# A widened 256-byte tile, one modulation vector moved to the tensor engine, and a gate unit moved into attention

## The chip, the cores and the metric

The kernel runs on one core of a Trainium2 chip. The metric is device microseconds of one execution, the median over the runs of a kernel. All arithmetic is in fp32, and the large matmuls use the fp32r form (one pass over split operands, see below).

## The reference

Two layers (DEPTH = 2) over 256 latent tokens x and 256 context tokens ctx, D_MODEL = 1024. Both streams pass layer 0; in layer 1 the context only gives keys and values. Cut to what matters here:

```
sh1, sc1, g1, sh2, sc2, g2 = split(silu(c) @ w_mod[l] + b_mod[l], 6)     # the same for c_ctx
xn   = rmsnorm(h, norm1_g[l]) * (1 + sc1) + sh1
proj = xn @ w_in[l]                  # pool | hyena | q | kv | gates ga, gb, gc (3 x 1024)
a    = pool_mixer(proj) @ pool_out
b    = hyena_mixer(proj) @ hy_out
cm   = attention(8 heads; latents read ctx and latent keys) @ w_o
h    = h + g1 * ((sigmoid(ga) * a + sigmoid(gb) * b + sigmoid(gc) * cm) @ w_out)
h    = h + g2 * (square(relu((rmsnorm(h, norm2_g[l]) * (1 + sc2) + sh2) @ w_ff1)) @ w_ff2)
```

So each layer needs six modulation vectors of 1024 numbers, each a product of a 1 x 1024 vector (per stream) with a 1024 x 1024 block of w_mod. The kernel numbers them 0 to 11 over both layers.

## The kernel before, in words

**Units.** Every large weight is cut into units of 128 x 1024 numbers (512 KB); there are 272, `PHASES` gives each phase its first unit `g0` and its count `mains`. SP loads a unit into one of four slots of `raw`; ScalarE copies it rounded into `wh` (line 750), VectorE writes the remainder `raw - wh` into `wl` (line 1078). That pair is called the split of the unit, done `AHEAD = 3` units before the unit is multiplied. TensorE multiplies a unit as 24 matmuls: for each of 8 blocks of 128 rows, high weight by high activation, high by low, low by high (`three`, lines 1629 to 1631). The activations are kept as such pairs too: `xh`/`xl` (the normed input), `hid_h`/`hid_l` (hidden layer of the MLP), `fh`/`fl` (attention output, pooled and hyena mix), `cqh`/`cql`, `ckh`/`ckl` (latents), `uh`/`ul`. A matmul has 512 columns in layer 0 (both streams) and 256 in layer 1.

**Tiles.** Tiles are placed one behind the other in the order of their `alloc` lines; the first starts at byte 8320 of a partition and each start is rounded up to 32 bytes. `h`, `xh`, `xl`, `raw`, `wh`, `wl` come first and start at multiples of 64 bytes. Then comes `picks`, `(36,)` floats (144 bytes), and behind it all other tiles; they start 32 bytes past a multiple of 64. In layer 1, `xh`, `xl`, `fh`, `fl`, `hid_h` and `hid_l` are read 192 bytes (3 x 64) further on (`by_layer`).

**Modulation vectors.** Vectors 0 and 1 are made at the start, the other ten in 80 units of w_mod (8 a vector), woven into the phases by the pattern strings in `_phases`: M is a main unit, m a modulation unit behind it, t one in the tail of the phase, s the sum of a weighed vector. A modulation unit on TensorE (`mod_unit`, line 1658) is four concurrent matmuls of 32 stationary columns. The vectors named in `SUMMED = (7, 8, 9)` are instead weighed on VectorE (`weigh`, lines 1099 and 1102: weight times the number of the partition, added into an accumulator in `gained` or `final`), and TensorE only sums the accumulator over the partitions with `picks` (`mod_sum`, line 1670). After either, ScalarE copies the rows ("copy", `copy_mod`), TensorE turns them ("turn", `turn_mod`, line 1677) and VectorE adds the bias (`add_mod`, line 1107). The tail units of `w_out` and of layer 0's `ff2b` run while the norm that follows is computed: TensorE does the squares' sum (`rms`), then the tail; meanwhile ScalarE takes the root, VectorE the reciprocal (line 1134), the products (line 1156) and the remainders `xl` (line 1163), and TensorE then starts the next phase with two units interleaved block by block (`wave`). Layer 0's `ff2b` has 8 tail units, all of them (`GAP_SLOTS`) loaded beforehand into free tiles, four of them into the room of `xl`, so that the first product of the norm waits for those four (`GAP_XL_LAST`).

**Attention.** The third gate has 8 units; `gate_c0` (4) stands before the projections uq and ukv, `gate_c1` (4) right before attention. ScalarE drains each gate unit by a sigmoid into `sig`, from PSUM banks 0 and 1. Attention has 16 jobs in layer 0 (8 heads x 2 streams; the context's see 256 keys) and 8 in layer 1. A job is: scores (line 1976), maxima on VectorE (1380), exponentials on ScalarE (960), division on VectorE (1387, 1390), transposes on TensorE (1987), copies on ScalarE (971); every two jobs one product with the values (`weighted_values`, 2002) into bank `pair % 2`, which VectorE drains to `fh`/`fl` (1401, 1402). In the last two jobs no scores are left to put between. Then comes `wo` (4 units in two halves of 12 matmuls each; VectorE drains by line 1427), then `pool`.

Of the kernel before, what the change touches and what calls it, by code (L numbers as in the profile page):

```python
# [7 lines left out]
KB = D // 128  # L8
# [49 lines left out]
def _phases():  # L58


    out = []
    for layer in range(DEPTH):
        first = layer == 0

        def with_mods(pattern):
            return pattern if first else pattern.replace("m", "").replace("t", "").replace("s", "")
        out += [(layer, *p) for p in [
            ("q", "MMM"), ("kv", "MM"), ("kpe", "M"),
            ("gate_c0", "MMMM"),
            ("uq", "MMM"), ("ukv", "MM"), ("gate_c1", "MMMM"),  # L70
            ("wo", with_mods("MMmmMMmm")),
            ("pool", with_mods("MMmmMMmm")),
            ("gate_a0", with_mods("MMmm")), ("gate_a1", with_mods("MMmmM")), ("pool_w", "M"),
            ("gate_a2", with_mods("MMmmMmm")), ("pool_out", "MMMM"),
            ("hy", with_mods("MMmmMMmmMMmmMMmmMMMM")), ("gate_b0", "MMM"), ("gate_b1", "MMM"), ("gate_b2", "MM"),
            ("hy_out", "MMMM"),
            ("w_out", "MMMMMMMM" + (16 if first else 8) * "t"),
            ("ff1a", with_mods("MMMMMMMMMMMMMMMM")), ("ff2a", with_mods("MmMmMmMmMmMmMmMmMmMmMmMmsMmMmMmMm")),
            ("ff1b", 16 * "M"), ("ff2b", with_mods("MmMmMmMmsMmMmMmMmMMMMsMMMM" + 8 * "t")),
        ]]  # L80
    return out
# [22 lines left out]

SUMMED = (7, 8, 9)

# [55 lines left out]
def load_order(order):  # L162
# [3 lines left out]
    for kind, i in order:  # L166
# [5 lines left out]
        else:  # L172
# [4 lines left out]
            else:  # L177
# [10 lines left out]
GAP_FREE = {"w_out": "hy_out", "ff2b": "ff2b"}  # L188
GAP_SLOTS = {i: (layer, name, slot) for layer, name, count in ((0, "w_out", 14), (0, "ff2b", 8), (1, "w_out", 6))
             for slot, i in enumerate(gap_units(layer, name, count))}  # L190
GAP_COUNTS = {(0, "w_out"): 14, (0, "ff2b"): 22, (1, "w_out"): 28}
GAP_XL_LAST = max(i for i, (_, name, slot) in GAP_SLOTS.items() if name == "ff2b" and slot < 4)
# [42 lines left out]
def backbone(nc, x_in, units_in, pairs_in, mod_units_in, params_in, consts_in, fwd_in, inv_in, counts_in, emb_in, f_w12_in,  # L235
# [5 lines left out]
    with ctx:  # L241
# [23 lines left out]
        wl = alloc(ctx, "wl", (SLOTS, 1024), R)  # L265
        picks = alloc(ctx, "picks", (36,))
        sq_sum = alloc(ctx, "sq_sum", (T,))
# [138 lines left out]
        with ExitStack() as s:  # L406
# [5 lines left out]
        weighted_of = {7: gained[:, :, :].rearrange("p a b -> p (a b)").rearrange("p (s c) -> p s c", c=D),  # L412
                       8: final[:, 0:1, :], 9: final[:, 1:2, :]}

# [6 lines left out]
        def latent_bank(i):  # L421

            p = PHASES[1, "q"]
            return (2 + p.dve0 % 2, 2 + (p.dve0 + 1) % 2, 6, 0, 1)[i]

        def pooled_bank(p, g):
# [306 lines left out]
        def _(act):  # L733
# [87 lines left out]
            def gates(layer, b, rest=None):  # L821
                p = PHASES[layer, "gate_" + b]
                n = width(layer)
                m0 = GATE_PARTS[b]
                for j in range(p.mains):
                    split(p.g0 + j + AHEAD)
                    act.wait_ge(unit_done, p.g0 + j + 1)
                    act.activation(sig[:, m0 + j, 0:n], ps[:, (p.act0 + j) % 2, 0:n], ACT.Sigmoid).then_inc(act_bank_free, 1)  # L828
                    if rest is not None:
                        rest(p, j)  # L830
                    mod_events(p, j)
# [92 lines left out]
            for layer in range(DEPTH):  # L924
# [39 lines left out]
                for jb, (hd, s) in enumerate(jobs):  # L964
                    if jb + 1 < len(jobs):
                        exponentials(jb + 1)
                    act.wait_ge(transposed[layer], jb + 1)
                    if jb >= 3:
                        act.wait_ge(pv_done[layer], (jb - 1) // 2)
                    for half in range(2 if jobs[jb][1] == 0 else 1):  # L970
                        act.activation(probs_t[jb % 3][:, 2 * half:2 * half + 2, :],
                                       ps[:, 6 + half, :].rearrange("p (k q) -> p k q", q=SEQ), ACT.Copy).then_inc(pt_act[layer], 1)
                for _ in straight(layer, "wo"):
                    pass
# [89 lines left out]
        def _(dve):  # L1064
# [44 lines left out]

            def loop(layer, name, drain=None):  # L1110
                p = PHASES[layer, name]
                for j in range(p.mains):
                    split(p.g0 + j + AHEAD)
                    if drain is not None:
                        drain(p, j)
                    mod_events(p, j)
# [158 lines left out]
            for layer in range(DEPTH):  # L1275
# [83 lines left out]
                for b in range(2):  # L1359
                    dve.tensor_tensor(roped[:, 0, b, :], q_pe[:, b, 0:SEQ], cos[:, :], ALU.mult)  # L1360
                    chained(dve.tensor_tensor(roped[:, 1, b, :], ps[:, 6, b * SEQ:(b + 1) * SEQ], sin[:, :], ALU.mult))
                    for i in range(4):
# [5 lines left out]
                        else:  # L1368
                            chained(done)
                loop(layer, "gate_c1")  # L1370

# [21 lines left out]
                def outputs(jb):  # L1393

                    hd, s = jobs[jb]
                    if hd % 2:
                        pair = jb // 2
                        dve.wait_ge(pv_done[layer], pair + 1)
                        src = ps[:, pair % 2, 0:SEQ]
                        t = slice(s * SEQ, (s + 1) * SEQ)  # L1400
                        chained(dve.tensor_copy(fh_of[layer][:, hd // 2, t], src))
                        dve.tensor_tensor(fl_of[layer][:, hd // 2, t], src, fh_of[layer][:, hd // 2, t].bitcast(F), ALU.subtract)\
                           .then_inc(o_ready[layer], 1)
# [11 lines left out]
                for jb in range(len(jobs) - 2, len(jobs)):  # L1415
                    outputs(jb)

                def branch_out(name, b):
# [207 lines left out]
        def _(pe):  # L1626
# [94 lines left out]

            def loop(layer, name, main, j0=0):
                p = PHASES[layer, name]
                for j in range(j0, p.mains):
                    pe.wait_ge(lo_ready, p.g0 + j + 1)
# [52 lines left out]
            def gates(layer, b, rest=None):  # L1778
                n = width(layer)

                def main(p, j):
                    bank = act_bank(p, j)
                    blocks(ps[:, bank, 0:n], (p.g0 + j) % SLOTS, xh_of[layer], xl_of[layer], n).then_inc(unit_done, 1)
                    if rest is not None:
                        rest(j)
                loop(layer, "gate_" + b, main)

# [98 lines left out]
            for layer in range(DEPTH):  # L1886
# [103 lines left out]
                def weighted_values(pair):  # L1990
# [4 lines left out]
                    if pair == 0:  # L1995
                        pe.wait_ge(act_bank_free, drained(layer, "gate_c1"))
                    elif pair >= 2:
                        pe.wait_ge(o_ready[layer], pair - 1)
                    pe.wait_ge(pt_act[layer], copies(jb + 1))
                    for kb in range(nb):  # L2000
                        for half in range(2):
                            mm = pe.matmul(ps[64 * half:64 * half + 64, pair % 2, 0:SEQ],  # L2002
                                           v_t[:, tb0 + kb, (hd - 1 + half) * VH:(hd + half) * VH],
# [3 lines left out]
                def copies(jb):  # L2007

                    return 2 * min(jb, HEADS) + max(jb - HEADS, 0)

                pe.wait_ge(q_ready, layer + 1)
# [8 lines left out]
                for jb in range(len(jobs)):  # L2020
                    if jb + 2 < len(jobs):
                        scores(jb + 2)
                    transposes(jb)
                    if jb >= 2 and jb % 2 == 0:
                        weighted_values(jb // 2 - 1)
                weighted_values(len(jobs) // 2 - 1)

# [7 lines left out]

                branch_out("wo", o_ready[layer], HEADS // 2 * (ns - 1))
                for j, p, slot in straight(layer, "pool"):
                    bank = act_bank(p, j)
# [276 lines left out]
```

## Time and profile before

| | us |
|---|---|
| median of 3 runs | 1378.83 (1377.84 to 1378.91) |
| profiled execution | 1376.82 |
| its span, first to last instruction | 1375.0 |
| TensorE busy | 1344.5 (98%) |
| VectorE busy | 818.0 (59%) |
| ScalarE busy | 550.3 (40%) |
| GpSimd busy | 198.3 (14%) |
| mean DMA rate | 149 GB/s |

The granted clock of TensorE is 0.998 of full speed over the span. A row of a timeline gives the start in us from the span's start, the duration, the engine, the line, the operation, the tiles it writes and reads, and, in brackets, idle time before it and what ended it. Matmuls overlap, so what a matmul costs the stream is the distance from its start to the start of the next, not its duration.

### The profile page before, as it was taken

To read this page: it belongs to the slowest core of one execution; us is meant where nothing else is said; L and a number is where in the kernel's file an instruction comes from. 1 tells how busy PE (TensorE), PEld (TensorE's weight loads), DVE (VectorE), ACT (ScalarE), POOL (GpSimd) and SP (SyncE) were. 2 spreads that over 40 slices of the span, in tenths; PEclk is the share of its full clock that TensorE was granted. 3 is DMA by queue.
4 is the path that set the end of the run, shared out by engine and by line. 5 is a ranking of instruction groups with operands and counts; after the bars stand their busy time and mean duration, and the time that the engine had idled before them with its cause. 6 is when DMAs were issued, how large, how long until landed. Compare 5 with 4: busy or idle time off the path is not lost.

```text
span 1375.0 us, 19372 instructions
## 1 busy us (share of the span) xinstructions
PE 1344.5 (98%) x7918; PEld 1104.8 (80%) x7918; DVE 818.0 (59%) x1163; ACT 550.3 (40%) x852; POOL 198.3 (14%) x177
## 2 busy tenths in 40 slices
PE   8999999999999999999999999999999999999998
PEld 3567766777777886888878887788779999899998
DVE  5576574234448666545644445378865788765663
ACT  6652462332233323443113331144555445553553
POOL 1261000703100142000000002300004404100012
PEclk9999999999999999999999999999999999999999
DMA  9342204444531363223553337314225647455552
GB/s 373 135 144 92 107 1 148 155 173 149 209 110 57 127 245 123 99 101 125 192 185 111 105 140 269 114 51 156 94 92 179 228 137 281 148 186 186 185 185 77
DMA packets 55433, 205.27 MB, mean 149 GB/s; under 512 B 6277, under 2 KB 6661, under 8 KB 53808
## 3 DMA queue, kind: packets, MB, share of 16 engines
q1 hardware_dynamic: 52848, 193.70, 40.5%
q0 software_dynamic: 2208, 9.81, 1.9%
q8 instruction: 63, 1.03, 0.3%
q10 hardware_dynamic: 288, 0.52, 0.1%
q14 instruction: 26, 0.21, 0.1%
HBM read 200.86 MB, written 3.15 MB: 148 GB/s over the span
## 4 chain that ended last, share of the span: by engine, by line
PE 89%; DVE 5%; ACT 2%; DMA 1%; issue 1%; SPq 0%; POOL 0%; DVEq 0%; ACTq 0%
PE ps L1629 27%; PE ps L1630 26%; PE ps L1631 26%; PE ps L1976 2%; DVE wl L1078 2%; PE ps L1987 1%; PE ps L2002 1%; DMA pairs<-in_pairs 1%; PE ps L1658 1%; PE ps L2074 1%; PE ps L2086 1%; PE ps L1818 1%; PE ps L1697 1%; DVE rstd L1134 1%; DVE k_t L1352 0%
## 5 line engine op out<-in xcount | busy, mean ns | idle before, releaser
L1629 PE MATMUL ps<-xh,wh 128*128 128x512 f32 (+2 forms) x1392 | 473.0, 340 | 2.9 <-DVE xl L1163 2.0
L1630 PE MATMUL ps<-xl,wh 128*128 128x512 f32 (+2 forms) x1392 | 465.4, 334 | 0.0
L1631 PE MATMUL ps<-xh,wl 128*128 128x512 f32 (+2 forms) x1392 | 465.4, 334 | 0.0
L1078 DVE TENSOR_TENSOR wl<-raw,wh 128x1024 fp32r<-128x1024 f32 (+2 forms) x272 | 353.4, 1302 | 175.2 <-ACT wh L750 172.2
L750 ACT ACTIVATE wh<-raw 128x1024 fp32r<-128x1024 f32 (+2 forms) x272 | 283.8, 1044 | 313.2 <-PE ps L1631 312.8
L1629 PEld LDWEIGHTS ps<-xh,wh 128*128 128x128 f32 (+1 forms) x1392 | 261.1, 188 | 43.9 <-issue 14.0
L1631 PEld LDWEIGHTS ps<-xh,wl 128*128 128x128 f32 (+1 forms) x1392 | 260.5, 187 | 29.2
L1630 PEld LDWEIGHTS ps<-xl,wh 128*128 128x128 f32 (+1 forms) x1392 | 260.2, 187 | 28.3 <-issue 1.2
L1629 PE MATMUL ps<-hid_h,wh 128*128 128x512 f32 (+1 forms) x512 | 174.5, 341 | 0.0
L1630 PE MATMUL ps<-hid_l,wh 128*128 128x512 f32 (+1 forms) x512 | 173.8, 339 | 0.0
L1631 PE MATMUL ps<-hid_h,wl 128*128 128x512 f32 (+1 forms) x512 | 173.3, 338 | 0.0
L1631 PEld LDWEIGHTS ps<-hid_h,wl 128*128 128x128 f32 x512 | 96.9, 189 | 11.7
L1629 PEld LDWEIGHTS ps<-hid_h,wh 128*128 128x128 f32 x512 | 96.1, 188 | 12.7 <-issue 1.2
L1630 PEld LDWEIGHTS ps<-hid_l,wh 128*128 128x128 f32 x512 | 96.3, 188 | 11.5
L1600 DVE TENSOR_TENSOR relu<-relu 128x512 f32<-128x512 f32 (+1 forms) x64 | 35.7, 559 | 98.9 <-ACT relu L1045 98.9
L1045 ACT ACTIVATE relu<-ps 128x512 f32<-128x512 f32 (+1 forms) x64 | 31.4, 491 | 140.7 <-PE ps L1631 140.7
L1577 DVE SCALAR_TENSOR_TENSOR h<-ps,mods,h 128x256 f32<-128x256 f32 x72 | 32.6, 481 | 88.9 <-PE ps L1631 88.8
L651 POOL TENSOR_TENSOR y<-y,gated 128x512 f32<-128x512 f32 (+1 forms) x32 | 36.3, 1142 | 257.7 <-DVE gated L1427 257.5
L828 ACT ACTIVATE sig<-ps 128x512 f32<-128x512 f32 (+1 forms) x48 | 23.5, 491 | 122.2 <-PE ps L1631 122.2
L637 POOL TENSOR_TENSOR sq_sum<-h 128x512 f32<-128x512 f32 (+1 forms) x4 | 5.2, 1298 | 453.7 <-DVE h L1577 453.7
L1629 PE MATMUL ps<-fh,wh 128*128 128x512 f32 (+1 forms) x192 | 66.0, 344 | 1.0 <-DVE gated L1427 0.9
L1631 PE MATMUL ps<-fh,wl 128*128 128x512 f32 (+1 forms) x192 | 65.1, 339 | 0.0
(273 smaller groups left out, 1467.2 us busy)
## 6 DMA issues: line engine op xcount, KB each, us to landing
raw<-in_units SPq DMA_DIRECT2D x262, 512.0 KB, 3.3
mod_ring<-in_mod_units SPq DMA_DIRECT2D x52, 512.0 KB, 4.1
gap_hy<-in_mod_units SPq DMA_DIRECT2D x15, 512.0 KB, 4.8
pairs<-in_pairs SPq DMA_DIRECT2D x6, 1024.0 KB, 14.2
raw<-in_units SPq DMA_DIRECT2D x6, 384.0 KB, 3.1
h<-in_x SPq DMA_DIRECT2D x4, 512.0 KB, 7.8
mod_ring<-in_pairs SPq DMA_DIRECT2D x2, 1024.0 KB, 15.8
counts<-in_counts POOLq DMA_DIRECT2D x2, 1024.0 KB, 5.1
```

Source lines behind the costliest of these rows:

```text
L651: pool.tensor_tensor(y[:, m, 0:n], y[:, m, 0:n], gated[:, m % 2, 0:n], ALU.add).then_inc(y_added[layer], 1)
L750: act.activation(wh[:, g % SLOTS, 0:n], raw[:, g % SLOTS, 0:n], ACT.Copy).then_inc(hi_ready, 1)
L828: act.activation(sig[:, m0 + j, 0:n], ps[:, (p.act0 + j) % 2, 0:n], ACT.Sigmoid).then_inc(act_bank_free, 1)
L1045: act.activation(relu[:, j % 2, 0:n], ps[:, (p.act0 + j) % 2, 0:n], ACT.Relu).then_inc(act_bank_free, 1)
L1078: dve.tensor_tensor(wl[:, g % SLOTS, 0:n], raw[:, g % SLOTS, 0:n], wh[:, g % SLOTS, 0:n].bitcast(F), ALU.subtract)\
L1134: dve.reciprocal(rstd[:, t], rstd[:, t]).then_inc(rstd_ready, 1)
L1577: last = dve.scalar_tensor_tensor(h[:, m, t], ps[:, bank, t], mods[:, gate, m, s:s + 1], h[:, m, t], ALU.mult, ALU.add)
L1600: dve.tensor_tensor(relu2[:, j % 2, 0:n], relu[:, j % 2, 0:n], relu[:, j % 2, 0:n], ALU.mult)\
L1629: pe.matmul(dst, w_h, m_h, start=first, stop=False)
L1630: pe.matmul(dst, w_h, m_l, start=False, stop=False)
L1631: return pe.matmul(dst, w_l, m_h, start=False, stop=last)
L1976: pe.matmul(ps[:, S_BANKS[2 * (jb % 2) + qb], 0:keys], q_t[0:QK, hd, q0:q0 + 128], k_t[0:QK, hd, k0:k0 + keys], start=True, stop=True).the ...
```

## The change

Three things:

1. `picks` is 64 floats (256 bytes) instead of 36, so every tile behind it starts 96 bytes later, at a multiple of 64.
2. `SUMMED` is (7, 8). Vector 9 goes through TensorE as 8 modulation units, three of them inside layer 0's `ff2b` and five in its tail, which has 13 units (11 of them in prepared room, the first of which for `xl`'s room is the tail's third). The copies and turns of vectors 9 and 10 fall into layer 1's first phases.
3. The fourth unit of `gate_c1` leaves its place before attention. It is multiplied in pieces into bank 0: four blocks (12 matmuls) before the transposes of the last job but one, then in layer 0 two blocks before the last job's transposes and two behind them, in layer 1 four behind them. The product of the last pair but one goes to bank 4. ScalarE takes its sigmoid behind the attention's copies, and the split of unit `g0 + 6` (the third of `wo`) comes on ScalarE and on VectorE behind attention.

```diff
-            ("ff1b", 16 * "M"), ("ff2b", with_mods("MmMmMmMmsMmMmMmMmMMMMsMMMM" + 8 * "t")),
+            ("ff1b", 16 * "M"), ("ff2b", with_mods("MMMsMmmMMMmMMMMMMMMM" + 13 * "t")),
-SUMMED = (7, 8, 9)
+SUMMED = (7, 8)
-GAP_SLOTS = {i: (layer, name, slot) for layer, name, count in ((0, "w_out", 14), (0, "ff2b", 8), (1, "w_out", 6))
+GAP_SLOTS = {i: (layer, name, slot) for layer, name, count in ((0, "w_out", 14), (0, "ff2b", 11), (1, "w_out", 6))
...
-        picks = alloc(ctx, "picks", (36,))
+        picks = alloc(ctx, "picks", (64,))
...
+        def output_bank(layer, pair):
+
+            return 4 if pair == HEADS // 2 * (width(layer) // SEQ) - 2 else pair % 2
...
                 for j in range(p.mains):
+                    if b == "c1" and j == p.mains - 1:
+                        return
                     split(p.g0 + j + AHEAD)
...
+                act.wait_ge(unit_done, PHASES[layer, "gate_c1"].g0 + 4)
+                act.activation(sig[:, KB - 1, 0:n], ps[:, 0, 0:n], ACT.Sigmoid).then_inc(act_bank_free, 1)
+                split(PHASES[layer, "gate_c1"].g0 + 3 + AHEAD)
                 for _ in straight(layer, "wo"):
...
-                loop(layer, "gate_c1")
+                loop(layer, "gate_c1", count=3)
...
                 for jb in range(len(jobs) - 2, len(jobs)):
                     outputs(jb)
+                split(PHASES[layer, "gate_c1"].g0 + 3 + AHEAD)
...
                     if pair == 0:
-                        pe.wait_ge(act_bank_free, drained(layer, "gate_c1"))
+                        pe.wait_ge(act_bank_free, drained(layer, "gate_c1", 3))
+                    elif pair == len(jobs) // 2 - 2:
+                        pe.wait_ge(exp_done[layer], 2 * (len(jobs) - 1))
...
+                def last_gate(at, count):
+
+                    p = PHASES[layer, "gate_c1"]
+                    if at == 0:
+                        pe.wait_ge(lo_ready, p.g0 + 4)
+                        pe.wait_ge(o_ready[layer], len(jobs) // 2 - 3)
+                    mm = blocks(ps[:, 0, 0:n], (p.g0 + 3) % SLOTS, xh_of[layer], xl_of[layer], n, k0=at, count=count,
+                                first=at == 0, last=at + count == KB, at=128 * at)
+                    if at + count == KB:
+                        mm.then_inc(unit_done, 1)
...
                     if jb + 2 < len(jobs):
                         scores(jb + 2)
+                    if jb == len(jobs) - 2:
+                        last_gate(0, 4)
+                    elif jb == len(jobs) - 1 and layer == 0:
+                        last_gate(4, 2)
                     transposes(jb)
                     if jb >= 2 and jb % 2 == 0:
                         weighted_values(jb // 2 - 1)
+                if layer == 0:
+                    last_gate(6, 2)
+                else:
+                    last_gate(4, 4)
                 weighted_values(len(jobs) // 2 - 1)
...
                 branch_out("wo", o_ready[layer], HEADS // 2 * (ns - 1))
+                pe.wait_ge(act_bank_free, drained(layer, "gate_c1"))
```

## Rows read from the trace of the kernel before

**Rows 1.** The page: busy time by engine; the chain that ended last.
```profile
PE 1344.5 (98%) x7918; PEld 1104.8 (80%) x7918; DVE 818.0 (59%) x1163; ACT 550.3 (40%) x852; POOL 198.3 (14%) x177
...
PE 89%; DVE 5%; ACT 2%; DMA 1%; issue 1%; SPq 0%; POOL 0%; DVEq 0%; ACTq 0%
```

**Rows 2.** Timeline of TensorE, layer 0, ff1b into ff2b (start, duration, operation).
```profile
801.23 0.39 PE L1629 MATMUL ps<-xh,wh 128*128 128x512 f32 x1
...
812.11 0.40 PE L1629 MATMUL ps<-hid_h,wh 128*128 128x512 f32 x1
...
817.73 0.39 PE L1629 MATMUL ps<-hid_h,wh 128*128 128x512 f32 x1
```

**Rows 3.** Timeline of TensorE, layer 0, values of ukv (weights as moving tile).
```profile
134.93 0.40 PE L1630 MATMUL ps<-wl,ckh 128*128 128x512 f32 x1
...
137.27 0.40 PE L1631 MATMUL ps<-wh,ckl 128*128 128x512 f32 x1
```

**Rows 4.** Timeline of TensorE, layer 1, first matmuls of units: gate_c1; ff2a, ff1b.
```profile
973.96 0.28 PE L1629 MATMUL ps<-xh,wh 128*128 128x256 f32 x1
...
976.68 0.28 PE L1629 MATMUL ps<-xh,wh 128*128 128x256 f32 x1
...
1271.98 0.28 PE L1629 MATMUL ps<-hid_h,wh 128*128 128x256 f32 x1
...
1274.86 0.28 PE L1629 MATMUL ps<-xh,wh 128*128 128x256 f32 x1
...
1277.68 0.28 PE L1629 MATMUL ps<-xh,wh 128*128 128x256 f32 x1
```

**Rows 5.** Timeline of TensorE, layer 0, end of attention and start of wo.
```profile
205.24 0.60 PE L1987 MATMUL ps<-consts,probs 128*128 128x128 f32 x4
207.20 0.66 PE L1987 MATMUL ps<-consts,probs 128*128 128x128 f32 x4 [1.36 <-DVE probs L1390]
...
209.50 0.66 PE L1987 MATMUL ps<-consts,probs 128*128 128x128 f32 x4 [0.63 <-DVE probs L1390]
210.94 1.08 PE L2002 MATMUL ps<-probs_t,v_t 128*64 128x256 f32 x8 [0.78 <-ACT probs_t L971]
211.95 0.51 PE L1629 MATMUL ps<-fh,wh 128*128 128x512 f32 x1
```

**Rows 6.** Waits of TensorE, 900 to 1375 us (total, times, longest).
```profile
PE ps L1987 <- ACT probs_t L971: 1.3, 1, 1.3
PE ps L2002 <- ACT probs_t L971: 1.3, 1, 1.3
```

**Rows 7.** Timeline of ScalarE and VectorE, layer 1, around attention.
```profile
985.45 1.28 ACT L960 ACT_TABLE_LOAD   x1
...
1017.89 1.22 DVE L1078 TENSOR_TENSOR wl<-raw,wh 128x1024 fp32r<-128x1024 f32 x1
1019.03 0.42 DVE L1427 TENSOR_TENSOR y<-ps,sig 128x256 f32<-128x256 f32 x1
```

**Rows 8.** Timeline of TensorE: two modulation units in wo; sum and turn in ff2b.
```profile
223.39 1.07 PE L1658 MATMUL ps<-mod_ring,silu_wide 128*32 128x256 f32 x16
...
880.88 0.64 PE L1670 MATMUL ps<-final,picks 128*32 128x256 f32 x8
...
887.17 0.51 PE L1677 MATMUL ps<-consts,mod_rows 128*128 128x8 f32 x4
```

**Rows 9.** Timeline of TensorE: the tail of ff2b and the wave behind it.
```profile
907.33 1.93 PE L1658 MATMUL ps<-gap_xl,silu_wide 128*32 128x256 f32 x32
909.08 1.91 PE L1658 MATMUL ps<-gap_relu,silu_wide 128*32 128x256 f32 x32
911.61 0.35 PE L1629 MATMUL ps<-xh,wh 128*128 128x256 f32 x1 [0.62 <-DVE xl L1163]
...
917.68 0.28 PE L1629 MATMUL ps<-xh,wh 128*128 128x256 f32 x1
```

**Rows 10.** Timeline of VectorE: the first products of that norm.
```profile
909.80 0.88 DVE L1156 SCALAR_TENSOR_TENSOR normed<-h,scales,rstd 128x256 f32<-128x256 f32 x2
```

More of the change, by code:

```diff
@@ L188 @@
 GAP_FREE = {"w_out": "hy_out", "ff2b": "ff2b"}
-GAP_SLOTS = {i: (layer, name, slot) for layer, name, count in ((0, "w_out", 14), (0, "ff2b", 8), (1, "w_out", 6))
+GAP_SLOTS = {i: (layer, name, slot) for layer, name, count in ((0, "w_out", 14), (0, "ff2b", 11), (1, "w_out", 6))
              for slot, i in enumerate(gap_units(layer, name, count))}
-GAP_COUNTS = {(0, "w_out"): 14, (0, "ff2b"): 22, (1, "w_out"): 28}
+GAP_COUNTS = {(0, "w_out"): 14, (0, "ff2b"): 25, (1, "w_out"): 31}
 GAP_XL_LAST = max(i for i, (_, name, slot) in GAP_SLOTS.items() if name == "ff2b" and slot < 4)
@@ L412, in backbone @@
         weighted_of = {7: gained[:, :, :].rearrange("p a b -> p (a b)").rearrange("p (s c) -> p s c", c=D),
-                       8: final[:, 0:1, :], 9: final[:, 1:2, :]}
+                       8: final[:, 0:1, :]}
         S_BANKS = (4, 5, 2, 3)
@@ L1108, in add_mod, with loop @@
                                   b_mod[:, v, :, :].rearrange("p (j b) s -> p j b s", b=2), ALU.add).then_inc(mod_ready, 1)
-            def loop(layer, name, drain=None):
+            def loop(layer, name, drain=None, count=None):
                 p = PHASES[layer, name]
-                for j in range(p.mains):
+                for j in range(p.mains if count is None else count):
                     split(p.g0 + j + AHEAD)
@@ L1398, in outputs @@
                         dve.wait_ge(pv_done[layer], pair + 1)
-                        src = ps[:, pair % 2, 0:SEQ]
+                        src = ps[:, output_bank(layer, pair), 0:SEQ]
                         t = slice(s * SEQ, (s + 1) * SEQ)
@@ L1720, in wave, with loop @@
                     wave_step(layer, k, units, n, ready)
-            def loop(layer, name, main, j0=0):
+            def loop(layer, name, main, j0=0, count=None):
                 p = PHASES[layer, name]
-                for j in range(j0, p.mains):
+                for j in range(j0, p.mains if count is None else count):
                     pe.wait_ge(lo_ready, p.g0 + j + 1)
@@ L1785, in main @@
                         rest(j)
-                loop(layer, "gate_" + b, main)
+                loop(layer, "gate_" + b, main, count=3 if b == "c1" else None)
             def warm(count):
@@ L2001, in weighted_values @@
                         for half in range(2):
-                            mm = pe.matmul(ps[64 * half:64 * half + 64, pair % 2, 0:SEQ],
+                            mm = pe.matmul(ps[64 * half:64 * half + 64, output_bank(layer, pair), 0:SEQ],
                                            v_t[:, tb0 + kb, (hd - 1 + half) * VH:(hd + half) * VH],
```

## The prediction, made before the changed kernel was run

> **What bounds the kernel now.** First the page: TensorE is busy 98% of the span and 89% of the chain that ended last is its work, VectorE's share of it is 5% [rows 1]. So time can be won in two ways only: TensorE's stream gets denser, or its few waits are filled. How dense it is shows in the timeline, from the start of one unit to the start of another. In layer 0, 48 matmuls on `xh`/`xl` take from 801.23 to 812.11, 10.88 us or 226.7 ns each; the 24 behind them, the same shape on `hid_h`/`hid_l`, take 5.62 us or 234.2 ns each [rows 2]. The same difference shows elsewhere: the 48 on `fh`/`fl` between 211.95 and 223.39 take 11.44 us, 234 ns each if 0.2 us goes to the change of kind at either end [rows 5, 8]. And in ukv, where `wh`/`wl` is the moving tile and `ckh` the stationary one, ten take 2.34 us, 234 ns each [rows 3]. What do the matmuls at 234 ns share? Not the engine's condition, for they follow those at 227 at once, and not the moving tile alone. Every matmul at 227 reads two tiles that lie ahead of `picks`, at multiples of 64 bytes; every one at 234 reads at least one tile behind it, 32 bytes off.
>
> In layer 1 a matmul has 256 columns and there are three paces: `xh` at 2.72 us a unit (113.3 ns) in gate_c1, `xh` at 2.82 (117.5 ns) in ff1b, `hid` at 2.88 (120 ns) in ff2a [rows 4]. The same tiles run at two paces there, so something beyond the address counts, and I have no row that says what picks between them.
>
> The waits: at the end of layer 0's attention TensorE idles 1.36, 0.63 and 0.78 us [rows 5], at the end of layer 1's 1.3 and 1.3 [rows 6].
>
> **The wide tile.** 36 floats are 144 bytes, rounded up to 160; 64 are 256. Everything behind `picks` moves by 96 bytes and then lies at a multiple of 64, in both layers, since the layers' shift is 192 bytes. `fh`, `fl`, `hid_h` and `hid_l` get the same remainder by 256 as `xh` and `xl` have in the same layer. I take the price of `xh` for them. Layer 0: wo, pool_out, hy_out (4 units each) and ff2a, ff2b (16 each) are 44 units at 24 x (234.2 - 226.7) = 0.18 us, 7.9 us. uq, ukv and pool_w are 114 more matmuls, worth 0.9 at most; as ukv waits for VectorE in between I count 0.5. Layer 1: the same 44 units. If they go to the slower pace of `xh`, 2.88 - 2.82 = 0.06 each, 2.6 us; if to the faster one, 0.16 each, 7.0. I take the slower, because ff2a follows ff1a and wo comes before units of the slower pace, and 0.2 for uq and ukv. Sum **-11.2**. Bounds: no change at all (0, a rival below), and -20: 7.0 instead of 2.6, and 41 `xh` units (pool, two gates, ff1a, ff1b) that run at 2.82 now falling to 2.72, another 4.1.
>
> The Trainium skill ("TensorE: Matmul & The Clock Gate", Step-by-step) speaks against this whole term: streamed matmuls follow each other in N/2.4 GHz plus about 2.5 ns, 215.7 for 512 columns, and the weights' load has a read port of its own that takes nothing from the running matmul. By it the tile's place is worth nothing. Neither 226.7 nor 234.2 is that number.
>
> **Vector 9.** VectorE loses eight weighings; ff2b runs without gaps on TensorE, so that buys nothing. TensorE loses one sum (0.64) and one turn (0.51) from ff2b and gains two units behind the turn of vector 8 (1.07), one alone (0.54 and 0.1 for the change of kind), and a turn in layer 1 (0.51) [rows 8]: +1.0. The tail grows from 8 to 13 units. Four take 1.75 us, 0.44 each, so from 907.33 the tail ends at 913.0 and the wave starts there, not at 911.61 [rows 9]: +1.4. The wave itself took 6.07 us where 48 matmuls at 117.5 ns are 5.64; the 0.4 are waits for `xl`, and with the products ahead by then they go. The first product now waits for the tail's sixth unit, 907.33 + 6 x 0.44 = 909.97, against 909.80 [rows 10]; the wave came 1.8 us behind the product, 911.8, which is still before 913.0. On SP, the loads of vector 11's first two units now wait for the tail's first two; behind them stand units that are needed some ten us later. ScalarE's copy of vector 10 waits for vector 9's turn, with the split of the next units queued behind it; these belong to gate_c0, behind kv and kpe. I count both at nothing; if that cover failed, a split (1.22 on VectorE, rows 7) would be late once. Sum **+2.0**, bounds +1.0 and +3.5.
>
> **The gate unit.** Layer 0: 5.44 us leave the stream ahead of attention (half of 10.88). Inside, TensorE goes from the transposes at 205.24 to wo at 211.95 in 6.71 us, of which 2.77 are waits [rows 5]. The three pieces are 12, 6 and 6 matmuls, 5.44 us, and six changes of kind, 0.6. The first piece is 2.7 us in a hole of 1.4, and what it delays closes the holes behind it; without any wait the stretch is 6.71 - 2.77 + 6.04 = 10.0, but the usual 0.1 to 0.2 between semaphore and start that was in those waits stays at two places, so 9.6 to 10.1. Net -5.44 + 3.1 = -2.3. Layer 1: 2.72 us leave. The pieces are 1.36 each with 0.2 for the changes of kind, in waits of 1.3 each [rows 6]: +0.5. Attention starts at gate_c1's end. There VectorE has three splits in a row to do and ScalarE the table load for the exponentials (1.28, rows 7), both now closer to the first maxima: +0.2.
>
> At attention's end ScalarE now has a table load (1.28), the sigmoid and the split of wo's third unit to do, and VectorE that split (1.22) before the one it did already, and only then its first drain of wo. Before, VectorE began wo's fourth unit's split at 1017.89 and the drain at 1019.03 [rows 7]; now the drain comes some 1.2 us later. In layer 1 half a unit of wo is 1.44 us and there are two banks, so the third half needs that drain 2.9 us after wo's start, about 1020: +0.8 us, between 0 and 1.3. In layer 0 the halves are 2.8 us and nothing waits. The raw slot of pool's third unit is free only after that split; its load has two units of wo to land in. The later table load of the gates falls away, where it was hidden. Layer 1 sum: -2.7 + 0.5 + 0.2 + 0.8 = -1.2. Together **-3.5**, bounds -5.5 (all hidden) and -1.5.
>
> **Sum.** -11.2 + 2.0 - 3.5 = -12.7. The profiled execution took 1376.82, which gives 1364.1; the median of the runs is 2.0 above it, 1378.83, which gives **1366.1**.
>
> **Rivals.** (a) Layer 1 falls into the faster pace, in its 44 units and in the `xh` units behind them: a further 4.4 + 4.1, 1357.6, halves of it likewise. For it: 2.72 on `xh` at the same remainders [rows 4]. Against: 2.82 on the same tiles in ff1b. 22%.
> (b) The place in the partition's lower or upper part decides, or the skill's rule holds and the difference has another cause, and the wide tile brings nothing: 2.0 - 3.5 = -1.5, 1377.3. For it: the tiles read at 227 ns all lie low, those at 234 all high, and no row has a low tile off the 64 or a high one on it. 8%.
> (c) The gate in attention gains nothing, as the pieces delay the last jobs and the late split holds up wo in both layers: 1369.6. 6%.
> (d) Slower: what counts is how the tiles lie to each other, and the new places are bad ones for ff2 and wo. The place is each of their matmuls, the price up to that between the fastest and the slowest pace in layer 1, 6.7 ns (113.3 to 120), for 2112 matmuls: +14, less 1.5, 1391. It decides from 0.7 ns a matmul on. Against it: `xh`, `xl`, `wh` and `wl` all have one remainder by 256 in layer 0 and are the fastest. 4%.
> The forecast as it stands has 60%.
>
> **How the numbers follow.** The time is the forecast's, 1366.1. The range must hold (a) in good part and (c): 1358 to 1372; it leaves out (b), (d) and the end of (a). A measurement of this kernel tells about 0.2%, 2.8 us, from no change. (b) is within it, (d) above, the rest below: faster 0.89, same 0.07, slower 0.04.
>
> **What will show it.** Right: a unit on `hid_h` in layer 0 takes 5.44 us from start to start, one on `fh` too; in layer 1 2.82 or 2.72. From gate_c1's end to wo's start layer 0 is some 3.1 us longer and layer 1 about 0.7, each less the unit that left. The tail of ff2b has 13 units and the wave starts 5.7 us behind its start. In layer 1 wo's third half waits for VectorE by up to 1 us. Wrong: `hid` units still at 5.62, or `xh` units that are no longer at 5.44; waits on modulation units for their loads in ff2b; a second wait in wo, or one in gate_c0, that was not there.

## The result and the profile after

| | before | after |
|---|---|---|
| median, us | 1378.87 (1377.84 to 1379.84, 4 runs) | **1365.86** (1365.22 to 1366.25, 4 runs) |
| ratio | | 0.9905, 95% [0.9888, 0.9922] |
| profiled execution; its span | 1376.82; 1375.0 | 1365.22; 1363.1 |

The forecast was 1366.1. The page of the changed kernel, busy time and chain, against [rows 1]:

```profile
PE 1337.0 (98%) x7974; PEld 1103.5 (81%) x7974; DVE 808.6 (59%) x1155; ACT 550.6 (40%) x852; POOL 194.9 (14%) x177
...
PE 91%; DVE 4%; ACT 2%; DMA 1%; issue 1%; POOL 0%; DVEq 0%; ACTq 0%; POOLq 0%
```

TensorE does 56 matmuls more in 7.5 us less of busy time: its stream is denser. Where: the first matmuls of the units from ff1b into ff2b in layer 0, and from ff2a into ff1b in layer 1 (TensorE's timeline; start, duration, operation), against [rows 2, 4].

```profile
798.73 0.39 PE L1639 MATMUL ps<-xh,wh 128*128 128x512 f32 x1
...
804.17 0.39 PE L1639 MATMUL ps<-hid_h,wh 128*128 128x512 f32 x1
...
809.61 0.39 PE L1639 MATMUL ps<-hid_h,wh 128*128 128x512 f32 x1
...
1260.94 0.28 PE L1639 MATMUL ps<-hid_h,wh 128*128 128x256 f32 x1
...
1263.76 0.28 PE L1639 MATMUL ps<-xh,wh 128*128 128x256 f32 x1
...
1266.59 0.28 PE L1639 MATMUL ps<-xh,wh 128*128 128x256 f32 x1
```

In layer 0 a unit on `hid_h` takes 5.44 us like one on `xh`, no longer 5.62: 226.7 ns a matmul, not 234.2. In layer 1 both take 2.83; before it was 2.88 on `hid_h`.

The end of attention in layer 0, against [rows 5]: L1997 are the transposes, L2014 the product with the values, L1639 on `xh` the pieces of the gate's unit.

```profile
199.90 0.60 PE L1997 MATMUL ps<-consts,probs 128*128 128x128 f32 x4
200.26 0.48 PE L1639 MATMUL ps<-xh,wh 128*128 128x512 f32 x1
...
203.12 0.60 PE L1997 MATMUL ps<-consts,probs 128*128 128x128 f32 x4
203.65 1.08 PE L2014 MATMUL ps<-probs_t,v_t 128*64 128x256 f32 x8
204.66 0.50 PE L1639 MATMUL ps<-xh,wh 128*128 128x512 f32 x1
...
206.15 0.60 PE L1997 MATMUL ps<-consts,probs 128*128 128x128 f32 x4
206.51 0.48 PE L1639 MATMUL ps<-xh,wh 128*128 128x512 f32 x1
...
208.08 1.08 PE L2014 MATMUL ps<-probs_t,v_t 128*64 128x256 f32 x8
209.09 0.50 PE L1639 MATMUL ps<-fh,wh 128*128 128x512 f32 x1
```

No row has a wait. From the transposes to wo it is 9.19 us, where it was 6.71 with 2.77 of waits. The pieces take 5.92 of it, from the start of each to the start of what follows it. In layer 1, against [rows 6]:

```profile
1003.00 0.36 PE L1639 MATMUL ps<-xh,wh 128*128 128x256 f32 x1
...
1004.55 1.95 PE L2014 MATMUL ps<-probs_t,v_t 128*64 128x256 f32 x16
1006.43 0.39 PE L1639 MATMUL ps<-fh,wh 128*128 128x256 f32 x1
...
1010.18 0.36 PE L1639 MATMUL ps<-fh,wh 128*128 128x256 f32 x1 [0.65 <-DVE y L1437]
```

The two waits of 1.3 us are gone, and the third half of wo now waits for VectorE's first drain. The tail of layer 0's ff2b and the wave behind it (TensorE, and VectorE's first products), against [rows 9, 10]:

```profile
897.24 1.07 PE L1668 MATMUL ps<-mod_ring,silu_wide 128*32 128x256 f32 x16
898.13 1.91 PE L1668 MATMUL ps<-gap_xl,silu_wide 128*32 128x256 f32 x32
899.85 3.21 PE L1668 MATMUL ps<-gap_relu,silu_wide 128*32 128x256 f32 x56
900.17 0.88 DVE L1165 SCALAR_TENSOR_TENSOR normed<-h,scales,rstd 128x256 f32<-128x256 f32 x2 [0.50 <-PE ps L1668]
...
902.99 0.39 PE L1639 MATMUL ps<-xh,wh 128*128 128x256 f32 x1
```

Thirteen units take 5.75 us, and the wave starts at their end with no wait of its own.

The phases of both kernels, from the end of one phase's last unit to the end of the next's, add up to this:

| part | before to after, us |
|---|---|
| layer 0, uq, wo, pool_out, hy_out | -0.4 -0.6 -0.6 -0.7 |
| layer 0, ff2a and ff2b's main units | -2.8 -2.8 |
| layer 0, gate_c1 and attention | -3.0 |
| vector 9: in ff2b, in layer 1's q and kpe | +0.7 +1.5 |
| layer 1, gate_c1, attention and wo | -1.8 |
| layer 1, ff2a, ff2b, hy_out, pool_out | -0.9 -0.9 -0.3 -0.1 |
| layer 1, pool, a0, a1, now at 2.72 us a unit | -1.0 |
| layer 1, c0, hy from its eighth unit on, b0, b1, now at 2.83 us a unit | +1.6 |

The sum is -12.1; the start of the program was 0.6 slower in this execution, and the two profiled executions lie 11.6 apart.

### The profile page after: what moved, and what is told of

The parts are those of the page before. It is cut to its first block, busy times and chain, and to the rows that moved or that the text cites. A ratio compares the mean times of both kernels' runs of the same rounds, so it can differ in the third digit from the quotient of the medians.

```text
span 1363.1 us, 19468 instructions
## 1 busy us (share of the span) xinstructions
PE 1337.0 (98%) x7974; PEld 1103.5 (81%) x7974; DVE 808.6 (59%) x1155; ACT 550.6 (40%) x852; POOL 194.9 (14%) x177
## 4 chain that ended last, share of the span: by engine, by line
PE 91%; DVE 4%; ACT 2%; DMA 1%; issue 1%; POOL 0%; DVEq 0%; ACTq 0%; POOLq 0%
PE ps L1639 27%; PE ps L1641 26%; PE ps L1640 26%; PE ps L1986 3%; PE ps L1668 1%; PE ps L2014 1%; PE ps L1997 1%; DVE wl L1087 1%; PE ps L2106 1%; PE ps L2118 1%; DVE rstd L1143 1%; DMA consts<-in_consts 1%; PE ps L1828 1%; DVE k_t L1361 0%; DMA raw<-in_units 0%
## 5 line engine op out<-in xcount | busy, mean ns | idle before, releaser
L1639 PE MATMUL ps<-xh,wh 128*128 128x512 f32 (+2 forms) x1392 | 473.4, 340 | 2.5 <-DVE xl L1172 1.5
L1639 PEld LDWEIGHTS ps<-xh,wh 128*128 128x128 f32 (+1 forms) x1392 | 260.3, 187 | 43.7 <-issue 13.6
L1639 PE MATMUL ps<-hid_h,wh 128*128 128x512 f32 (+1 forms) x512 | 172.1, 336 | 0.0
L1639 PEld LDWEIGHTS ps<-hid_h,wh 128*128 128x128 f32 x512 | 96.1, 188 | 11.5 <-issue 1.6
L1639 PE MATMUL ps<-fh,wh 128*128 128x512 f32 (+1 forms) x192 | 65.3, 340 | 1.8 <-DVE gated L1437 1.0
L1640 PE MATMUL ps<-fl,wh 128*128 128x512 f32 (+1 forms) x192 | 64.1, 334 | 0.0
```

The costliest lines, as they stand in the source:

```text
L1639: pe.matmul(dst, w_h, m_h, start=first, stop=False)
L1640: pe.matmul(dst, w_h, m_l, start=False, stop=False)
```

## The experiments

Ratios are to runs of the kernel before beside them, with 95% intervals. "Distance" means here: start of the moving tile (`xh`, `hid_h`, `fh`) less start of the weights' tile `wh`, as a remainder by 256 bytes. In the kernel before it is 0 for `xh` and 160 for `hid_h` in layer 0, 192 and 96 in layer 1; in the changed kernel 0 for all three in layer 0 and 192 for all three in layer 1. A "pace" is the mean distance from one matmul's start to the next inside a unit; a unit is 24 of them.

**The wide tile alone**, in the kernel before:

```diff
-        picks = alloc(ctx, "picks", (36,))
+        picks = alloc(ctx, "picks", (64,))
```

> The kernel before with the wide tile alone (36 to 64 floats). Theory: the remainder by 64 bytes of the tiles that TensorE reads sets its pace; -11 us against before (the changed kernel's phases say about -0.18 us per layer 0 unit on hid or fh and -0.06 in layer 1), units on hid_h in layer 0 at 5.44 us. Rival, the gain came from the other two edits: within 2 us of before.

1369.03 us (1367.32 to 1370.86, 4 runs), ratio 0.9933 [0.9918, 0.9949]. Layer 0 gains 8.3 behind its q, 8.1 of it in the phases that read tiles behind `picks`, ff2a and ff2b 2.8 each. In layer 1 the tiles behind `picks` gain 2.2 (ff2a and ff2b 0.86 each), but gate_c1, hy, b0 and b1, all on `xh`, lose 2.8: they go from 2.72 to 2.83 us a unit, and one unit of hy starts 0.8 late.

**A multiple of 64 that is not one of 256**, in the kernel before: (36,) becomes (44,), and the tiles behind start at a multiple of 64 bytes, at distance 192 in layer 0 and 128 in layer 1.

> The kernel before with picks at 44 floats: the tiles behind it start 32 bytes later, at a multiple of 64 but with another remainder by 128 and 256 than in the changed kernel. If the multiple of 64 is all that counts: hid units in layer 0 at 5.44 us and about -11 us. If it must be 128 or 256 bytes: between 0 and -11, hid units at some pace between 5.44 and 5.62.

1373.95 us (1372.86 to 1375.41, 9 runs), ratio 0.9974 [0.9964, 0.9983]. Two units of ff2b in layer 0 and two of ff2a in layer 1:

```profile
812.13 0.39 PE L1629 MATMUL ps<-hid_h,wh 128*128 128x512 f32 x1
...
817.74 0.39 PE L1629 MATMUL ps<-hid_h,wh 128*128 128x512 f32 x1
...
1264.90 0.28 PE L1629 MATMUL ps<-hid_h,wh 128*128 128x256 f32 x1
...
1267.78 0.28 PE L1629 MATMUL ps<-hid_h,wh 128*128 128x256 f32 x1
```

5.60 us a unit (from 817.74 to 823.34 again 5.60), hardly less than 5.62, and 2.88 as before. The rule "multiple of 64 bytes" is wrong. Layer 0 gains only about 1 us in this trace. Layer 1's `xh` units gain more, as pool, a0, a1 and ff1b run at 2.72 here (-2.6) while b0 and b1 run at 2.83 (+0.6), and its ff2b runs at 118.7 ns a matmul, 2.85 us a unit (-0.5), though it has the same distance as ff2a.

**Every tile off the 64.** The changed kernel with 32 bytes ahead of `h`: all large tiles start 32 bytes past a multiple of 64, and no distance changes.

```diff
+        alloc(ctx, "off", (8,))
         h = alloc(ctx, "h", (KB, T))
```

> The changed kernel with 32 bytes put ahead of its first tile, so that h, xh, xl, raw, wh, wl and all others are 32 bytes off a multiple of 64. If the remainder counts: units on xh in layer 0 go from 5.44 to about 5.62 (some 86 full units of layer 0, 16 us, less where they wait) and hid goes back to 5.62; layer 1 slower too; about +25 us against the changed kernel, 1391. If the place in the lower or upper part counts: as the changed kernel, 1366.

1366.02 us (1365.81 to 1366.49, 4 runs), ratio 0.9916 [0.9903, 0.9930]: the changed kernel's time. Units of ff1b and ff2b in layer 0:

```profile
798.93 0.39 PE L1640 MATMUL ps<-xh,wh 128*128 128x512 f32 x1
...
804.37 0.39 PE L1640 MATMUL ps<-hid_h,wh 128*128 128x512 f32 x1
...
809.81 0.39 PE L1640 MATMUL ps<-hid_h,wh 128*128 128x512 f32 x1
```

5.44 us on both. A start at a multiple of 64 is not needed for the fast pace. The time is also what the lower or upper part would give, the other reading named above. That reading falls by other runs: with the wide tile `hid_h` runs at 5.44 and still lies in the upper part, and in the next kernel `xh`, in the lower part, runs at 5.62.

**The weights moved away.** The changed kernel with 96 bytes ahead of `wh`, and `picks` cut so that what lies behind it stays. In layer 0 `xh` and `hid_h` are then at distance 160.

```diff
+        alloc(ctx, "off", (24,))
         wh = alloc(ctx, "wh", (SLOTS, 1024), R)
         wl = alloc(ctx, "wl", (SLOTS, 1024), R)
-        picks = alloc(ctx, "picks", (64,))
+        picks = alloc(ctx, "picks", (40,))
```

> The changed kernel with wh and wl alone 96 bytes further on (picks gives the 96 bytes back, so that all other tiles stay). New theory: what counts is the distance, modulo 256 bytes, between the moving tile and the tile that the weights are loaded from; 0 gives 226.7 ns a matmul of 512 columns, 160 gave 234.2. Here it is 160 for every large matmul: units on xh as well as on hid in layer 0 go to 5.62 us, +16 us or so in layer 0 and some 3 to 10 in layer 1, about 1385 to 1392. Rival, the remainder of each tile by itself: xh and hid keep their addresses and at most a part of it is lost; within 3 us of 1366.

1395.68 us (1394.35 to 1396.65, 4 runs), ratio 1.0138 [1.0123, 1.0153]. Units of ff1b and of ff2b:

```profile
812.09 0.40 PE L1640 MATMUL ps<-xh,wh 128*128 128x512 f32 x1
...
817.71 0.40 PE L1640 MATMUL ps<-xh,wh 128*128 128x512 f32 x1
...
823.34 0.40 PE L1640 MATMUL ps<-hid_h,wh 128*128 128x512 f32 x1
...
828.96 0.39 PE L1640 MATMUL ps<-hid_h,wh 128*128 128x512 f32 x1
```

Both now take 5.62 us. `xh`, which ran at 5.44 in every kernel so far, has not moved against anything but the weights. With the run before, in which all tiles moved together and nothing changed, this settles it: the pace goes with where the moving tile lies **to the weights' tile**. It makes this kernel 29.8 us slower than the changed one. That is more than was expected, as layer 0 lost some 20 us behind ukv, and layer 1 another 9.4 with every unit at 2.88.

One rival is left: `wh` and `wl` are also where ScalarE and VectorE write, so TensorE might be held up by their writes and not by its own reads. The trace speaks against it. In ff1b the matmuls during which a split is written follow each other in 234.3 ns, those during which ScalarE, VectorE and GpSimd all stand still in 234.3 too (128 and 126 of them). `raw`, where the DMA writes, has not moved against `xh`.

**Only the low weights moved**: the same 24 floats between `wh` and `wl`.

> The changed kernel with wl alone 96 bytes further on. By the theory of the distance only the matmuls are late during which wl is read: if it is the load of the next weights that meets the running matmul's moving tile, the second of each three (moving xl or hid_l while wl is loaded) or its neighbour is longer, and a unit of layer 0 lies between 5.44 and 5.62 us, at about 5.50. If all three are equally late (5.62), the load is not what meets. If none is, the theory falls.

1384.38 us (1383.63 and 1385.12, 2 runs), ratio 1.0056 [1.0034, 1.0078]. One matmul in three reads `wl`, and the unit loses most, not a third, of the 0.18 us:

```profile
813.35 0.40 PE L1640 MATMUL ps<-xh,wh 128*128 128x512 f32 x1
...
818.94 0.39 PE L1640 MATMUL ps<-hid_h,wh 128*128 128x512 f32 x1
```

5.59 us. The delay is spread over all three kinds of matmul (228 to 236 ns; the means in ff1b are 233.2, 231.7 and 232.9 in the order of `three`). By the sign set before the run that speaks against the load of the next weights as the one thing that meets the running matmul, but it does not show what does. Which of TensorE's reads disturbs which stays open.

**Layer 1 at other distances.** `SHIFT` sets how far on `xh`, `fh` and `hid` are read in layer 1: 192 bytes as it stands. It was set to 0 in the changed kernel, and to 64 and 224 bytes in the kernel with vector 9 on VectorE (below).

```diff
-SHIFT = 48
+SHIFT = 0
```

> The changed kernel with layer 1's tiles at layer 0's places (shift 0 instead of 192 bytes). By the theory of the distance layer 1 then has distance 0 like layer 0: if 0 is best at 256 columns too, its units run at 2.72 us throughout, instead of 2.72 in some phases and 2.83 in others, and the time is 5 us lower. If 0 is bad for 256 columns, where loads and matmuls alternate twice as fast, units take 2.83 us or more throughout and it is some 5 us or more higher. I lean to the second, 60 to 40.

> The wide tile and the gate in attention, vector 9 on VectorE, with layer 1's tiles 64 bytes instead of 192 behind layer 0's. Measured so far at 256 columns: distance 0 gives 120 ns, 96 about 120, 192 gives 113.3 or 117.7. If the pace depends on the distance by its smallest residue (64 either way), 64 gives what 192 gives and the time stays at 1363; if the sense matters, some other pace between 113 and 120, at most 9 us more or, if it were 113.3 throughout, 5 us less. Layer 0 does not change.

> As layer1_shift_64, with 224 bytes. 32 bytes closer to distance 0 (256) than now: by a smooth dependence between 192 (113.3 to 117.7) and 0 (120), so slower than now by some 3 us, 1366. If only multiples of 64 can be at the better paces: 120 ns, 1371.

0: 1374.13 us (1372.72 to 1375.33, 10 runs), ratio 0.9978 [0.9969, 0.9988]. 64: 1366.25 (1365.16 to 1367.02, 4 runs), 0.9918 [0.9904, 0.9933]. 224: 1367.35 (1366.98 to 1367.76, 4 runs), 0.9927 [0.9911, 0.9944]. Two units each, at 0, at 64 and at 224 bytes:

```profile
1268.35 0.28 PE L1639 MATMUL ps<-hid_h,wh 128*128 128x256 f32 x1
...
1271.23 0.28 PE L1639 MATMUL ps<-xh,wh 128*128 128x256 f32 x1
```
```profile
1264.92 0.28 PE L1639 MATMUL ps<-xh,wh 128*128 128x256 f32 x1
...
1267.75 0.28 PE L1639 MATMUL ps<-xh,wh 128*128 128x256 f32 x1
```
```profile
1265.66 0.28 PE L1639 MATMUL ps<-xh,wh 128*128 128x256 f32 x1
...
1268.50 0.28 PE L1639 MATMUL ps<-xh,wh 128*128 128x256 f32 x1
```

2.88, 2.83 and 2.84 us a unit. At 64 bytes the faster pace that 192 also has never shows, so the two sides are not alike. At distance 0, the best in layer 0, layer 1 has its slowest pace everywhere. The unshifted `cqh` bears it out: at distance 0 its steady matmuls in layer 1 of the changed kernel run at 120 ns too. 192 bytes is the only distance at which units at 2.72 were seen. The table of the paces of `xh`, `fh` and `hid`, each a unit's time by 24:

| distance | 512 columns (layer 0), ns | 256 columns (layer 1), ns |
|---|---|---|
| 0 | 226.7 | 120.0 |
| 64 | | 117.8 |
| 96 | | 120.0 |
| 128 | | 120.0 or 118.7 |
| 160 | 234.2 | |
| 192 | 233.3 | 113.3 or 117.8 |
| 224 | | 118.3 |

**Vector 9 alone**, the change's second part in the kernel before:

```diff
-SUMMED = (7, 8, 9)
+SUMMED = (7, 8)
-             ... ("ff2b", with_mods("MmMmMmMmsMmMmMmMmMMMMsMMMM" + 8 * "t")),
+             ... ("ff2b", with_mods("MMMsMmmMMMmMMMMMMMMM" + 13 * "t")),
```

> The kernel before with vector 9 back on TensorE and nothing else. Theory: one microsecond more in ff2b's stream and one in the longer tail, +2.0 us against before. Rival (a faster VectorE frees something): 0 or below.

1380.14 us (1379.14 to 1383.09, 11 runs), ratio 1.0020 [1.0011, 1.0029]: +2.3. In its trace ff2b is 0.64 longer, layer 1's q 1.15 and kpe 0.38, the last being a turn.

**The other two parts without it**: the changed kernel with vector 9 back on VectorE (the same lines the other way).

> The changed kernel with vector 9 back on VectorE (wide tile and gate in attention). Theory: 2 us lower than the changed kernel, 1363.9. Rival: the three edits need each other and it is the same.

1363.13 us (1361.22 to 1363.73, 4 runs), ratio 0.9900 [0.9884, 0.9915]. Against the changed kernel's trace, ff2b is 0.67 shorter, q 1.29, kv 0.32, kpe 0.37: 2.65 together. Some 0.5 of it is pace and not vector 9: the units of q and kv run at 113.3 ns a matmul here and at 117.8 in the changed kernel. Against the wide tile alone it gives the third part: from ukv's end to wo's end layer 0 is 2.95 shorter (91.34, not 94.29) and layer 1 is 2.0 (53.08, not 55.09). Of that 0.4 is pace: the unit that left would have taken 2.83 in the tile's kernel and not 2.72, and wo behind its wait runs at 113.3 ns, not 117.8.

**The split before attention.** In the kernel of the run before this one, with vector 9 on VectorE, the split of wo's third unit goes back to its old place, on ScalarE as shown and on VectorE likewise:

```diff
                 for j in range(p.mains):
+                    split(p.g0 + j + AHEAD)
                     if b == "c1" and j == p.mains - 1:
                         return
-                    split(p.g0 + j + AHEAD)
```

> The wide tile and the gate in attention, vector 9 on VectorE, with the split of wo's third unit ahead of attention on ScalarE and VectorE. It takes away the 0.8 us wait of layer 1's third half unit of wo, but then 1.05 us on ScalarE and 1.22 on VectorE stand between gate_c1's end and the first exponentials in both layers. If the latter are on the path: some 1.0 to 1.7 us more at each attention's start, 1.5 to 2.5 slower in sum. Rival, the split is hidden at the start as it was in the kernel before: 0.8 us faster.

1366.69 us (1363.31 to 1366.94, 4 runs), ratio 0.9917 [0.9902, 0.9931]. wo's wait is gone (-0.79 in layer 1), but attention's start pays for it in the profiled execution, one of the three at 1366.7 to 1366.9. The scores of layer 0's second job, and TensorE's windows around them (us; busy and number; granted clock; DMA share; GB/s):

```profile
164.18 2.38 PE L1985 MATMUL ps<-k_t,q_t 96*128 96x512 f32 x4 [1.53 <-ACT probs L966]
```
```profile
162.00:164.00 2.00, 0.64 (x2) 1.00 0.42 119
164.00:168.00 4.00, 3.82 (x12) 0.71 0.18 72
168.00:172.00 4.00, 4.00 (x16) 0.87 0.00 0
```

The scores wait 1.53 us for exponentials that stand behind the split, and then the granted clock is 0.71 and 0.87 over the next eight us: transposes follow each other in 213 ns, not 109, which is the lower of the clock's two levels (1.2 GHz) and the upper (2.4). Layer 0 loses 3.0 by this, layer 1 1.3 less the 0.8; there the scores wait 1.3 us too, and the granted clock stays at 1.00. The fourth execution took 1363.31, with a mean clock of 0.998 where the others have 0.993 to 0.995: it seems to have been spared the slow stretch in layer 0, but it was not profiled. Putting the split behind attention is therefore right by the median; a wait of 1.5 us there cost twice itself where the clock fell with it.

**The split in between.** In the kernel with the wide tile and the gate alone, the split goes where both engines idle at attention's end: on ScalarE before its last copy of transposes, on VectorE ahead of the last drains.

```diff
                         exponentials(jb + 1)
+                    else:
+                        split(PHASES[layer, "gate_c1"].g0 + 3 + AHEAD)
                     act.wait_ge(transposed[layer], jb + 1)
...
-                split(PHASES[layer, "gate_c1"].g0 + 3 + AHEAD)
...
+                split(PHASES[layer, "gate_c1"].g0 + 3 + AHEAD)
                 for jb in range(len(jobs) - 2, len(jobs)):
                     outputs(jb)
-                split(PHASES[layer, "gate_c1"].g0 + 3 + AHEAD)
```

> The kernel with the wide tile and the gate in attention alone (1363.13), with the split of wo's third unit put into holes at attention's end: on ScalarE into the 1.82 us in which it idles before the copy of the last transposes in layer 1, on VectorE ahead of the last pairs' drains, where it idles 0.69 and 3.44 us. Theory: the split behind attention is what makes wo's third half wait in layer 1 (0.70 us), so that wait goes, nothing else moves, and the time is about 1362.4; in layer 0 nothing changes. Rival 1: what holds the third half is not this split but the two behind it on both engines, which move up with it, and the wait stays: 1363.1. Rival 2: the split delays a copy or a division of the last jobs, as the early split did with the first scores, and TensorE idles 0.5 to 1.5 us per layer there: 1364 to 1366.

**1361.18 us** (1360.37 to 1362.36, 4 runs), ratio 0.9885 [0.9868, 0.9901], the lowest of all. ScalarE and VectorE in layer 1: the split of wo's third unit, the product's drain, and wo's first two drains.

```profile
998.40 1.06 ACT L754 ACTIVATE wh<-raw 128x1024 fp32r<-128x1024 f32 x1
...
1000.12 1.22 DVE L1088 TENSOR_TENSOR wl<-raw,wh 128x1024 fp32r<-128x1024 f32 x1
...
1003.59 0.43 DVE L1411 CAST fh<-ps 128x256 fp32r<-128x256 f32 x1 [2.26 <-PE ps L2015]
...
1005.52 0.42 DVE L1438 TENSOR_TENSOR y<-ps,sig 128x256 f32<-128x256 f32 x1
...
1006.61 0.42 DVE L1438 TENSOR_TENSOR y<-ps,sig 128x256 f32<-128x256 f32 x1 [0.67 <-PE ps L1642]
```

The drain comes before the third half of wo needs it: wo is 0.80 shorter in layer 1 and nothing in attention is longer, as the theory had it. But the median fell by 2.0, not 0.8. The rest is in part pace: c0, hy, b0 and b1 ran at 2.72 us a unit in this kernel (-1.7), a2, b2 and hy_out a little slower (+0.7). The two profiled executions lie only 0.85 apart (1361.22 and 1360.37), since this one reached layer 0's gate_c1 1.1 later. Units of hy in layer 1, in this kernel and, earlier and later in the phase, in the changed one:

```profile
1084.02 0.28 PE L1640 MATMUL ps<-xh,wh 128*128 128x256 f32 x1
...
1086.74 0.28 PE L1640 MATMUL ps<-xh,wh 128*128 128x256 f32 x1
```
```profile
1079.13 0.28 PE L1639 MATMUL ps<-xh,wh 128*128 128x256 f32 x1
...
1081.85 0.28 PE L1639 MATMUL ps<-xh,wh 128*128 128x256 f32 x1
...
1087.80 0.28 PE L1639 MATMUL ps<-xh,wh 128*128 128x256 f32 x1
...
1090.63 0.28 PE L1639 MATMUL ps<-xh,wh 128*128 128x256 f32 x1
```

Same tiles, same distance of 192, 2.72 against 2.83 us. The changed kernel ran at 2.72 as well until a pause of TensorE at 1084.46 (0.44 us to the next start), and at 2.83 behind it. Only the 0.8 belongs to the edit by what was shown; its interval overlaps that of the kernel it was made from.

## Why the prediction was right, and which step of it was not

The median is 0.2 us from the forecast, the sign and the range hold. Between the two profiled executions the fall is 11.6, where 12.7 was forecast, with 0.6 lost at the start. That it came as close as 0.2 is luck: errors in both directions cancelled, and the reason given for the largest term was wrong. Term by term:

- **The wide tile, layer 0** (forecast -8.4): -8.3 in the trace of the tile alone. The price was taken from `xh` at the same remainder by 256, and that was the right row to take it from.
- **Its reason was wrong.** The step that failed is "Every matmul at 227 reads two tiles that lie ahead of `picks`, at multiples of 64 bytes; every one at 234 reads at least one tile behind it, 32 bytes off", taken as a rule on multiples of 64. A multiple of 64 left 5.60 us a unit, all tiles off the 64 left 5.44, and moving the weights alone made `xh` 5.62. What the runs showed in its place is the mechanism of rival (d), how the tiles lie to each other, with the other sign: the new places are good ones in layer 0. The prediction's argument against (d) named the right fact, one remainder for all. The forecast held because 256 bytes satisfy both rules at once; for 44 floats the multiple of 64 would have promised the same 11 us, and the kernel gained 3.9.
- **Layer 1** (forecast -2.8): the tiles behind `picks` gave -2.2 with the tile alone, at the slower of the two paces as chosen. Rival (a), the faster pace, came in the changed kernel in pool, a0, a1 and parts of wo, pool_out and hy_out; in ff1 and ff2 it did not come in any kernel but one (the multiple of 64, ff1b alone). Not forecast were the `xh` units that changed pace in both directions, +0.6 in the changed kernel, +2.0 and a late unit with the tile alone.
- **Vector 9** (forecast +2.0): +2.3 alone and +2.65 by phases in the changed kernel, some 0.5 of the latter by pace, inside the bounds. The tail's end was forecast at 5.7 us behind its start and came at 5.75; the wave took 5.76, not 6.07. ff2b itself lost 0.7 where 1.0 was charged, and layer 1's q and kpe lost 1.5, the longer tail less the wave's waits (+1.0 forecast) and a turn (0.5).
- **The gate's unit** (forecast -3.5): -3.0 in layer 0 and -1.6 in layer 1 once the units' pace is taken out, -4.6. Layer 0's stretch was forecast at 9.6 to 10.1 us and took 9.19. The pieces and their changes of kind cost 5.92 (charged 6.04). The three transposes and two products between them cost 3.27 from start to start, where the prediction had 3.94, the stretch less its waits. This is the term that it sized wrongly: a group in front of a wait counts there with its whole duration (0.60 us at 205.24), and in a stream that goes on it costs 0.36. In layer 1 the wait of wo's third half was forecast at 0.8 and is 0.8 from matmul to matmul (0.65 in its row). That it comes from the split behind attention was only argued; the last run shows it, as it goes when the split moves.
- Rival (b) fell with the wide tile alone, which brought `hid_h` in the upper part to 5.44 us, and with `xh` at 5.62 in the lower part when the weights moved. (c) fell with the trace of attention.
- **The skill's rule.** The Trainium skill ("TensorE: Matmul & The Clock Gate", Step-by-step) gives 215.7 ns from one streamed matmul of 512 columns to the next, and names no place of the tiles. The lowest pace of any run is 226.7, and places alone moved it to 234.2 and the kernel by 29.8 us. On this point the Trainium skill and the runs differ, and the runs decide.

So the sum was closer than its parts: the gate gave 1.1 more than forecast, layer 1's tiles 0.6 less, the other units' paces took 0.6, vector 9 a few tenths more.

## What to carry to other kernels

When one shape of matmul runs at two paces in a trace, list the starts of both its tiles and look at the remainder of their difference by 256 bytes. Try each width of matmul for itself: the best distance for 512 columns was the worst for 256. An edit that moves some tiles can be tested by moving the others, which costs two lines. A unit of independent work cut into pieces fills the waits at a pipeline's end, but the work queued behind it on the slower engines has to be put into their idle stretches as well.

## What the runs showed of the hardware that was not expected

- The pace of streamed matmuls depends on the distance of the moving tile from the weights' tile: 226.7 to 234.2 ns with 512 columns, 113.3 to 120.0 with 256. That the remainder by 256 is what counts fits every run. `xl` starts 16640 bytes behind `xh`, an odd multiple of 256, and both run alike (226.2 and 227.1 ns on `wh` in ff1b), so 512 is not the period. Moving `wl` alone slowed all three kinds of matmul.
- At a distance of 192 bytes 256 columns have two paces, 113.3 and 117.8 ns, and at 128 also two, 118.7 and 120.0 (ff2b and ff2a of one kernel). A pace is held over many units. The change comes where TensorE waits or changes its kind of work, inside a phase too, as in hy. What picks between them stays open; between the kernels measured it is worth up to about 2 us.
- A wait of TensorE of 1.5 us at attention's start in layer 0 was followed by a granted clock of 0.71 and 0.87 for some eight us, and cost 3.0 in all. The wait of 1.3 us at the same place in layer 1, and those of 1.3 us at attention's end in the kernel before, were followed by no such stretch.
